# State space mixer's gate product z as seven block products, and the scan's shared value turned once

## The chip, the cores and the metric

The kernel runs on one core of one Trainium2 chip. The metric is the device time of one execution in microseconds, as the median of the runs shown; lower is better. All data are float32. An engine's name stands for itself: TensorE (PE in the profile, with its weight loads as PEld), VectorE (DVE), ScalarE (ACT), GpSimd (POOL) and SyncE (SP).

## The reference, cut to what matters

Two blocks of a network work on 256 latent and 256 context tokens of width 1024. The change touches two mixers of the first block. The state space mixer has eight groups of four heads; z gates its output:

```python
def ssd_mixer(h_lat, h_ctx, ctx_out, w_in, conv_w, conv_b, dt_bias, a_log, d_skip, norm_g, w_out):
    ...
        z, xbc, dt = jnp.split(h @ w_in, [D_INNER, D_INNER + CONV_DIM], axis=-1)
        xbc = jax.nn.silu(dwconv_centred(xbc, conv_w, conv_b))
    ...
    def out(y, z):
        yg = y.reshape(bsz, n, D_INNER).astype(z.dtype) * jax.nn.silu(z)
        yn = rmsnorm(yg.reshape(bsz, n, SSD_GROUPS, D_INNER // SSD_GROUPS), ...)
        return yn.reshape(bsz, n, D_INNER) @ w_out
```

The other is a recurrent scan over the tokens in two directions; both directions read the same v:

```python
def wkv_bidir(prep, s0s):
    r, v, kk, _, dirs = prep
    (df, kf, bf), (db, kb, bb) = dirs
    yf, sf = wkv_scan(r, df, kf, v, kk, bf, s0s[0], False)
    yb, sb = wkv_scan(r, db, kb, v, kk, bb, s0s[1], True)
    return yf + yb, sf, sb
```

## The kernel before

Activations lie feature by feature on 128 partitions, tokens along the free axis. The weights come as 221 tiles of 1 MB in the order of the list PRODUCTS, through a ring of four; SyncE loads tile t when tile t - 4 has been used up (semaphore tiles_used). Products are written to two pairs of PSUM banks in turn; a product may start when the product two before it in the list has been read out, which the semaphores act_emptied and dve_emptied tell. Each engine runs one list of instructions, in the order in which the functions named `..._pe`, `..._dve`, `..._act` and `..._pool` issue them. A float32 matmul stands in the profile as two instructions.

**The state space mixer** (ssd_pe, ssd_dve, ssd_act, ssd_pool) runs one period for each group g. TensorE's list in a period: the first chunk of the product bc of group g + 1 (128 weight columns by 512 tokens, L1861), the decays of group g (L1899), the second chunk of bc (256 tokens), the turns of group g (L1912 to L1918; they wait for both minima and for ScalarE's silu of x and bc), the product z of group g (two chunks of eight matmuls by 256 tokens, L1861), the states and factor rows (L1929, L1938), the first chunk of x of group g + 1, the outputs (L1954 to L1964), the second chunk of x, and one matmul for the norm (L1973). In the last group there is no bc and no x to come: there the first chunk of z stands ahead of the decays, the second behind them, and the turns follow.

VectorE's list in a period: eight conv taps on x of group g (L2148, after ScalarE's copy L2049), the mix of group g - 1 (L2222, L2225, not in group 0), two minima (L2270, after TensorE's decays and a copy by ScalarE, L2094), eight taps on bc of group g + 1, the mask (L2276), four products for the weight matrix (L2281, L2284), the state decays (L2289, which TensorE's outputs wait for), and then, once TensorE's outputs are there (L2238 on), the gate with z's silu (L2251) and a sum (L2253) for the norm. ScalarE does the copies, exponentials, silus and the root; z's silu reads the finished product from PSUM (L2111). GpSimd scales the turned x (L2319) and prepares the next decays (L2309).

**Seven block products** is a form that the MLPs and one more product use already. A tile holds 1024 by 256 weights. Split in halves both ways, weights and tokens give a 2 by 2 block product that takes seven instead of eight block products, each of four matmuls of 128 by 128 weights by 128 tokens (seven_group_pe, L317). VectorE makes four sums of weight blocks beforehand (sums_dve, L368 to L374, each 512 columns; the semaphore mixed tells that they are there, and TensorE waits for it ahead of the third block product), four sums of token blocks once for an input (terms_dve, L390 to L395), and joins the results in four operations (join_dve, L423 to L432) after ScalarE has copied the first of them out of PSUM (first_out_act, L413).

**The scan** (rwkv_scan_pe and its fellows) has eight steps of 64 tokens in each of two directions; the second direction takes the chunks in the order 3, 2, 1, 0, 7, 6, 5, 4. In each step TensorE turns two arrays, V and Q, of each direction, by matmuls with the identity on 64 by 64 pieces (turns, turn_quad, L1432): 32 instructions for a direction. ScalarE copies the two out together, 512 columns (token_rows, L1591, recorded as L1586). Behind the turns stand products that wait for VectorE's transposes (L1679). FIRST_TOUCH = (0, 1, 4, 5) are the steps in which a chunk is met for the first time; in the others the other direction has turned it already.

Of the kernel before, what the change touches and what calls it, by code (L numbers as in the profile page):

```python
# [10 lines left out]
ACT = mybir.ActivationFunctionType  # L11
# [5 lines left out]
SEQ = 256  # L17
CTX = 256
# [23 lines left out]
    *[(f"ssd_{n}{g + d}", 1, 1, by) for g in range(G - 1)  # L42
      for n, d, by in (("bc", 1, "dve"), ("z", 0, "act"), ("x", 1, "dve"))],
    (f"ssd_z{G - 1}", 1, 1, "act"), ("ssd_out", 4, 2, "dve"),
    ("mlp1_up", 16, 1, "dve"), ("mlp1_down", 4, 4, "dve"),
# [168 lines left out]

SEVEN_RUNS = [("mlp0_up", "mlp0_down"), ("mlp1_up", "mlp1_down"), ("gate2", "up2", "down2"), ("hy_mix",)]
TOKENS = {"hy_mix": TOK, "mlp0_up": TOK, "mlp0_down": TOK}
MIX_RUN = 3
RUN_AT, RUN_TILES = {}, []
# [10 lines left out]
FIRST_OUT_AT = {}  # L229
for _run in SEVEN_RUNS[MIX_RUN:] + SEVEN_RUNS[:MIX_RUN]:  # L230
    for _n in _run:
        for _g in range(SHAPE_OF[_n][0]):
            FIRST_OUT_AT[_n, _g] = len(FIRST_OUT_AT) + 1
# [5 lines left out]
def seven_blocks(m, run, n):  # L239

    tile, kt = RUN_TILES[run][n]
    w = m.ring[:, tile % RING, :].rearrange("p (k c n) -> p k c n", k=8, n=P)
    half = kt // 2
    a = [[w[:, half * kh:half * kh + half, c, :] for kh in range(2)] for c in range(2)]
    return tile, half, a, [x[:, 0:half, :] for x in m.weight_sums[run in (1, 2)][n % 2]]

# [110 lines left out]
def sums_dve(s, m, run, n):  # L357

    if run == 0 and 2 <= n < 2 + SIDE_BLOCKS:
        side_block_dve(s, m, n - 2)  # L360
    if n >= len(RUN_TILES[run]):
        return
    dve, sem = s.eng, s.sem
    tile, _, a, w = seven_blocks(m, run, n)
    dve.wait_ge(sem[f"tile_in{tile % RING}"], (tile // RING + 1) * 16)
    if n >= 2:
        dve.wait_ge(sem["tiles_used"], RUN_TILES[run][n - 2][0] + 1)
    dve.tensor_tensor(w[0], a[1][0], a[1][1], ALU.add).then_inc(sem["dve_step"], s.one("dve_step"))  # L368
    dve.tensor_tensor(w[2], a[0][0], a[1][0], ALU.subtract)
    dve.wait_ge(sem["dve_step"], s.made("dve_step"))  # L370
    dve.tensor_tensor(w[1], w[0], a[0][0], ALU.subtract).then_inc(sem["dve_step"], s.one("dve_step"))
    dve.wait_ge(sem["dve_step"], s.made("dve_step"))
    if run or n < 16:
        dve.tensor_tensor(w[3], a[0][1], w[1], ALU.subtract).then_inc(sem["mixed"], s.one("mixed"))  # L374
    else:
        dve.tensor_tensor(w[3], a[0][1], w[1], ALU.subtract)
        b, t = down0_inputs(m, n - 16)
        terms_dve(s, b, t, "mixed")
# [19 lines left out]
def first_kept(m, name, g):  # L398

    if name == "mlp0_down":  # L400
        return m.first0[0]
    return m.first0[g % 2] if name in ("mlp0_up", "hy_mix") else m.first[g % 2]

def first_out_act(s, m, name, g):

    act, sem = s.eng, s.sem
    act.wait_ge(sem["first_done"], FIRST_OUT_AT[name, g])
    if name == "mlp0_down":
        act.wait_ge(sem["first_used"], FIRST_OUT_AT[name, g] - 1)  # L410
    elif g >= 2:
        act.wait_ge(sem["first_used"], FIRST_OUT_AT[name, g] - 2)
    act.activation(first_kept(m, name, g), seven_sums(m, name, g, FIRST), ACT.Copy).then_inc(sem["first_out"], 1)  # L413
# [448 lines left out]
def mlp1_up_dve(s, m):  # L862
    dve, sem = s.eng, s.sem
    hid = m.big_hidden(SEQ)
    dve.wait_ge(sem["h_ready"], s.next("h_ready", NORM_ACT * 2))
    dve.wait_ge(sem["h_rest"], s.made("h_rest"))
# [584 lines left out]
def rwkv_scan_pe(s, m):  # L1451
# [17 lines left out]
    def turns(n, ds):  # L1469
        for d in ds:  # L1470
            for hp in range(HP):
                for w, src in enumerate("VQ"):
                    ins = turn_quad(pe, m, m.place(d, 2, w, hp), chunk(n, d, src, hp))
            ins.then_inc(sem["rows_turned"], s.one("rows_turned"))
# [106 lines left out]
def rwkv_scan_act(s, m):  # L1581
# [6 lines left out]
    def token_rows(n, ds):  # L1588
        for d in ds:
            act.wait_ge(sem["rows_turned"], s.next("rows_turned"))  # L1590
            copy(m.tok_vq(d, n), m.half_bank(d, 2)).then_inc(sem["tok_out"], s.one("tok_out"))  # L1591

# [401 lines left out]
def ssd_pe(s, m):  # L1994
# [9 lines left out]
    for g in range(G - 1):  # L2004
# [3 lines left out]
        ssd_turn_pe(s, m, g)  # L2008
        for c in range(2):
            ssd_chunk_pe(s, m, f"ssd_z{g}", c, SEQ)  # L2010
        ssd_states_pe(s, m, g)
# [4 lines left out]
    g = G - 1  # L2016
    ssd_chunk_pe(s, m, f"ssd_z{g}", 0, SEQ)
    ssd_decays_pe(s, m, g)
    ssd_chunk_pe(s, m, f"ssd_z{g}", 1, SEQ)
    ssd_turn_pe(s, m, g)  # L2020
# [48 lines left out]
def ssd_act(s, m):  # L2069
# [17 lines left out]
    for g in range(G):  # L2087
# [20 lines left out]
        if g < G - 1:  # L2108
            conv_silu_act(s, m, f"ssd_bc{g + 1}", m.conv_bc(g + 1))
        wait_product(s, f"ssd_z{g}", 0)  # L2110
        act.activation(m.z_silu, m.pairs[:, GROUP_AT[f"ssd_z{g}", 0] % 2, :, 0:SEQ], ACT.Silu) \  # L2111
            .then_inc(sem["act_emptied"], s.one("act_emptied"))
        act.wait_ge(sem["new_state"], g + 1)
# [116 lines left out]
def ssd_gate_dve(s, m, g):  # L2230
# [18 lines left out]
    dve.tensor_tensor(y, y, far[:, 0, :], ALU.add).then_inc(sem["dve_step"], s.one("dve_step"))  # L2249
    dve.wait_ge(sem["dve_step"], s.made("dve_step"))  # L2250
    dve.tensor_tensor(m.y_now, m.y_now, m.z_silu, ALU.mult).then_inc(sem["y_gated"], 1)  # L2251
    dve.wait_ge(sem["ssd_squares"], g + 1)
    dve.tensor_tensor(m.y_sq[:, 0, :], m.y_sq[:, 0, :], m.y_sq[:, 1, :], ALU.add).then_inc(sem["y_gated"], 1)  # L2253

def ssd_dve(s, m):
    dve, sem = s.eng, s.sem
    ssd_dt_dve(s, m)
    conv_taps_dve(s, m, "ssd_bc0", bc_chunks(m, 0))
    ssd_tokens_dve(s, m)  # L2260
    dve.wait_ge(sem["ssd_consts"], 16)
    masks = m.ssd_masks.rearrange("p (d t) -> p d t", d=2)[:, None, :, :].broadcast_to([P, 2, 2, P])
    for g in range(G):
        conv_taps_dve(s, m, f"ssd_x{g}", x_chunks(m, g))
        if g:
            ssd_mix_dve(s, m, g - 1)
        for c in range(2):
            dve.wait_ge(sem["seg_kept"], 2 * g + c + 1)
# [9 lines left out]
        for c in range(2):  # L2278
# [5 lines left out]
            dve.tensor_tensor(w, w, m.cbm[:, c, 1:2, :].broadcast_to([P, HPG, P]), ALU.mult) \  # L2284
                .then_inc(sem["w_ready"], 1)
        dve.wait_ge(sem["state_out"], g + 1)
        for dr in range(2):
# [850 lines left out]
class Memory:  # L3138

    def __init__(self, nc, ctx):
# [241 lines left out]
    def tok_v(self, d, n):  # L3383
        return self.tok_vq(d, n)[:, 0:256].rearrange("p (h n) -> p h n", h=HP)

# [438 lines left out]
```

## Time and profile before

| | us |
|---|---|
| runs of the kernel before | 2139.05, 2139.24, 2146.56 |
| median | 2139.24 |
| profiled execution | 2142.77 |
| its span, first to last instruction | 2141.0 |
| TensorE busy in the span | 2091.7 (98%) |
| VectorE busy | 1271.6 (59%) |
| ScalarE busy | 512.0 (24%) |
| GpSimd busy | 159.9 (7%) |

The profiled execution is one of many and lies 3.5 us above the median of the runs. Its times start at the span's beginning. A duration in the timeline of TensorE runs to the modelled end of the last matmul in the row, so the start of the next row tells better how long the row kept TensorE.
### The profile page before, as it was taken

Reading aid. Unit: us, or ns where it says so; the run is one execution under the profiler, and the core shown is the slowest. Engines: PE = TensorE matmul, PEld = TensorE weight load, DVE = VectorE, ACT = ScalarE, POOL = GpSimd, SP = SyncE. Lnnn points to the kernel's source line nnn. Section 1 sums busy time; section 2 is a strip of 40 time slices with the busy share of each in tenths; the row PEclk is TensorE's granted clock in tenths of the full one; section 3 lists DMA queues with packets and bytes.
Section 4 is the critical chain, followed back from the end, with each engine's and each line's share of the span. In section 5 each row is a group of like instructions: output and inputs, shape, how many; then the busy total and the mean of one; then the engine's idle time right before and its main releaser. Section 6 shows DMA issues by size and latency. Waiting matters only on the chain.

```text
span 2141.0 us, 39541 instructions
## 1 busy us (share of the span) xinstructions
PE 2091.7 (98%) x17242; PEld 1701.4 (79%) x17242; DVE 1271.6 (59%) x2425; ACT 512.0 (24%) x1068; POOL 159.9 (7%) x180
## 2 busy tenths in 40 slices
PE   8999899999999999999999999999999999999999
PEld 5854688985588888885666667899998877789999
DVE  4647654444576778766555555388543554239874
ACT  2224732221200000004443444100012243402100
POOL 0002132220000000000221122000001000000000
PEclk9999999999999999999999999999999999999999
DMA  8221022211333334343221222445445522344543
GB/s 337 87 79 60 21 82 82 76 60 51 146 128 127 139 121 148 118 140 135 79 79 59 79 79 75 157 165 183 164 172 197 197 92 87 118 147 148 178 170 126
DMA packets 40693, 261.70 MB, mean 122 GB/s; under 512 B 4919, under 2 KB 6599, under 8 KB 11848
## 3 DMA queue, kind: packets, MB, share of 16 engines
q1 hardware_dynamic: 36720, 249.59, 32.3%
q10 hardware_dynamic: 2904, 6.40, 0.8%
q0 software_dynamic: 896, 3.18, 0.4%
q8 instruction: 136, 2.23, 0.4%
q14 instruction: 37, 0.30, 0.0%
HBM read 257.54 MB, written 1.08 MB: 121 GB/s over the span
## 4 chain that ended last, share of the span: by engine, by line
PE 54%; DVE 1%; ACT 0%; issue 0%; ACTq 0%; DVEq 0%
PE pairs L317 16%; PE pairs L1861 12%; PE pairs L186 9%; PE pairs L2898 4%; PE bank L317 3%; PE pairs L1988 1%; PE pairs L2826 1%; PE bank L1964 1%; PE bank L1954 1%; PE bank L2810 1%; PE bank L1929 1%; PE bank L1899 1%; PE bank L1938 0%; PE bank L2404 0%; PE bank L1912 0%; PE bank L1956 0%
## 5 line engine op out<-in xcount | busy, mean ns | idle before, releaser
L1861 PE MATMUL pairs<-h_sb,ring_sb 128*128 128x512 f32 (+1 forms) x784 | 264.3, 492 | 0.0
L1861 PEld LDWEIGHTS pairs<-h_sb,ring_sb 128*128 128x128 f32 x784 | 147.6, 191 | 105.6 <-issue 94.5
L186 PE MATMUL pairs<-h_sb,ring_sb 128*128 128x256 f32 (+1 forms) x720 | 221.6, 466 | 0.9 <-DVE h_sb L708 0.9
L186 PEld LDWEIGHTS pairs<-h_sb,ring_sb 128*128 128x128 f32 x720 | 135.3, 190 | 84.4 <-issue 72.7
L317 PE MATMUL pairs<-mid 128*128 128x128 f32 (+1 forms) x1304 | 197.1, 306 | 0.0
L317 PEld LDWEIGHTS pairs<-mid 128*128 128x128 f32 x1304 | 179.4, 191 | 10.1
L317 PE MATMUL bank<-mid 128*128 128x256 f32 x544 | 122.0, 379 | 0.0
L317 PE MATMUL pairs<-h_sb,ring_sb 128*128 128x128 f32 (+1 forms) x784 | 118.2, 303 | 3.3 <-ACT h_sb L622 2.7
L317 PEld LDWEIGHTS bank<-mid 128*128 128x128 f32 x544 | 103.4, 190 | 14.1
L317 PEld LDWEIGHTS pairs<-h_sb,ring_sb 128*128 128x128 f32 x784 | 105.8, 193 | 10.9 <-ACT h_sb L622 2.9
L368 DVE TENSOR_TENSOR mid<-ring_sb 128x512 f32<-128x512 f32 (+1 forms) x105 | 71.7, 683 | 67.5 <-PE pairs L317 40.1
L2148 DVE SCALAR_TENSOR_TENSOR big<-pairs,vec_table,big 128x508 f32<-128x508 f32 (+3 forms) x128 | 76.9, 675 | 51.3 <-ACT big L2049 51.2
L317 PE MATMUL pairs<-mid,ring_sb 128*128 128x128 f32 (+1 forms) x520 | 91.2, 318 | 0.0
L186 PE MATMUL pairs<-big,ring_sb 128*128 128x256 f32 x416 | 90.4, 379 | 0.5 <-DVE big L2963 0.5
L2898 PE MATMUL pairs<-h_sb,ring_sb 128*128 128x256 f32 x384 | 89.6, 383 | 0.0
L186 PEld LDWEIGHTS pairs<-big,ring_sb 128*128 128x128 f32 x416 | 79.0, 190 | 11.5 <-DVE big L2963 0.8
L317 PE MATMUL pairs<-big,ring_sb 128*128 128x256 f32 (+1 forms) x472 | 86.6, 331 | 0.0
L317 PEld LDWEIGHTS pairs<-mid,ring_sb 128*128 128x128 f32 x520 | 78.0, 191 | 5.6
L317 PEld LDWEIGHTS pairs<-big,ring_sb 128*128 128x128 f32 x472 | 75.0, 191 | 6.6
L2898 PEld LDWEIGHTS pairs<-h_sb,ring_sb 128*128 128x128 f32 x384 | 70.5, 190 | 12.3 <-issue 3.9
L317 PE MATMUL pairs<-big,mid 128*128 128x128 f32 x648 | 76.9, 275 | 0.0
L317 PEld LDWEIGHTS pairs<-big,mid 128*128 128x128 f32 x648 | 74.6, 192 | 0.0
(550 smaller groups left out, 3617.2 us busy)
## 6 DMA issues: line engine op xcount, KB each, us to landing
ring_sb<-weights SPq DMA_DIRECT2D x221, 1024.0 KB, 4.8
lora_w<-side SPq DMA_DIRECT2D x32, 512.0 KB, 3.3
x_sb<-tokens ACTq DMA_DIRECT2D x1, 2048.0 KB, 12.1
mid<-bias_table POOLq DMA_DIRECT2D x1, 1536.0 KB, 6.9
const_table<-consts ACTq DMA_DIRECT2D x1, 1200.0 KB, 9.0
const_table<-cond_rows SPq DMA_DIRECT2D x1, 1024.0 KB, 10.8
mid<-bias_table POOLq DMA_DIRECT2D x1, 1024.0 KB, 12.7
out<-x_sb ACTq DMA_DIRECT2D x4, 256.0 KB, 2.6
```

The source lines that it names most:

```text
L186: last = pe.matmul(out, w[:, k, c, :], rhs(j * kt + k), start=(j == 0 and k == 0), stop=(j * kt + k == k_end - 1))
L317: ins = pe.matmul(seven_sums(m, name, g, place), left[:, k, :], right[:, k, :], start=(j == 0 and k == 0), stop=(j == tpg - 1 and k == hal ...
L368: dve.tensor_tensor(w[0], a[1][0], a[1][1], ALU.add).then_inc(sem["dve_step"], s.one("dve_step"))
L1861: ins = pe.matmul(m.pairs[:, at % 2, c, 0:T], w[:, k, c, :], m.h[:, k, TOK - T:TOK], start=(k == 0), stop=(k == 7))
L1899: ins = pe.matmul(m.bank[:, 2 * c + dr, :], m.cs_keys[rows, CTX + c * L:CTX + c * L + L], m.cs_heads[c][rows, :], start=True, stop=True)
L1929: ins = pe.matmul(m.bank[:, 0, SEQ * dr:SEQ * dr + SEQ], m.b_tok[:, tt, :], m.xdt_end[:, dr, tt, :], start=(tt == 0), stop=(tt == 1))
L1954: pe.matmul(out, m.states[:, far, dr, cols], lat, start=True, stop=not far)
L1964: ins = pe.matmul(m.bank[64 * side:64 * side + 64, 3, SEQ * j + P * c:SEQ * j + P * c + P], m.xdt[:, dr, c, 64 * h:64 * h + 64], m.wmat[:, ...
L1988: ins = pe.matmul(m.pairs[:, at % 2, c, 0:SEQ], w[:, k % 8, c, :], m.y_fm[:, k, :], start=(k == 0), stop=(k == 15))
L2148: ins = dve.scalar_tensor_tensor(out[:, :, a:b], src[:, :, a + o:b + o], m.vec("conv_w")[:, k + 32 * tap:k + 32 * tap + 1], out[:, :, a:b] ...
L2810: ins = pe.transpose(m.bank[0:n, 2 + side, at:at + P], m.probs2[:, t % 2, side, lo:lo + n], m.const("ident"))
L2898: ins = pe.matmul(m.pair4[:, 2 + g % 2, c * SEQ:c * SEQ + SEQ], w[:, k, c, :], m.h[:, k, CTX:TOK], start=(k == 0), stop=(k == 7))
```

## The change

The product z becomes a fifth run of seven block products (Z_RUN) with sums, terms and a first product of its own in SBUF. VectorE makes the four sums for z of group g behind the mix and ahead of the minima; a sum may start when the tile of z of the group before has been used. It makes the four terms once, ahead of the first x taps, and the join behind the weight matrix' products, ahead of the state decays. ScalarE copies the first product where silu was; silu now runs in place on the joined z behind the exponentials of the factors, and the gate waits for it. In the last group TensorE issues the decays after the fourth block product. In the scan V is turned and copied only in the steps of FIRST_TOUCH, and the other steps read the copy that the other direction made. The second MLP's wait for h_ready is split in two, since the mixer now waits for the first half of its count.

```diff
-      for n, d, by in (("bc", 1, "dve"), ("z", 0, "act"), ("x", 1, "dve"))],
-    (f"ssd_z{G - 1}", 1, 1, "act"), ("ssd_out", 4, 2, "dve"),
+      for n, d, by in (("bc", 1, "dve"), ("z", 0, "dve"), ("x", 1, "dve"))],
+    (f"ssd_z{G - 1}", 1, 1, "dve"), ("ssd_out", 4, 2, "dve"),
-SEVEN_RUNS = [("mlp0_up", "mlp0_down"), ("mlp1_up", "mlp1_down"), ("gate2", "up2", "down2"), ("hy_mix",)]
+SEVEN_RUNS = [("mlp0_up", "mlp0_down"), ("mlp1_up", "mlp1_down"), ("gate2", "up2", "down2"), ("hy_mix",),
+              tuple(f"ssd_z{g}" for g in range(G))]
@@ sums_dve
+    kept = 1 if run == Z_RUN else 2
+    if n >= kept:
+        dve.wait_ge(sem["tiles_used"], RUN_TILES[run][n - kept][0] + 1)
@@ mlp1_up_dve
-    dve.wait_ge(sem["h_ready"], s.next("h_ready", NORM_ACT * 2))
+    dve.wait_ge(sem["h_ready"], s.next("h_ready", NORM_ACT))
@@ rwkv_scan_pe, turns
-                for w, src in enumerate("VQ"):
-                    ins = turn_quad(pe, m, m.place(d, 2, w, hp), chunk(n, d, src, hp))
+                if n in FIRST_TOUCH:
+                    turn_quad(pe, m, m.place(d, 2, 0, hp), chunk(n, d, "V", hp))
+                ins = turn_quad(pe, m, m.place(d, 2, 1, hp), chunk(n, d, "Q", hp))
@@ rwkv_scan_act, token_rows
-            copy(m.tok_vq(d, n), m.half_bank(d, 2)).then_inc(sem["tok_out"], s.one("tok_out"))
+            if n in FIRST_TOUCH:
+                copy(m.tok_v(d, n), m.part(d, 2, 0))
+            copy(m.tok_q(d, n), m.part(d, 2, 1)).then_inc(sem["tok_out"], s.one("tok_out"))
+def ssd_z_pe(s, m, g, between=None):
+    pe, sem = s.eng, s.sem
+    if g == 0:
+        pe.wait_ge(sem["terms"], s.next("terms", 4))
+    seven_group_pe(s, m, f"ssd_z{g}", 0, lambda j: (halves(m.h[:, :, CTX:TOK], 0, 4), m.z_terms), between=between)
@@ ssd_pe
-        for c in range(2):
-            ssd_chunk_pe(s, m, f"ssd_z{g}", c, SEQ)
+        ssd_z_pe(s, m, g)
...
     g = G - 1
-    ssd_chunk_pe(s, m, f"ssd_z{g}", 0, SEQ)
-    ssd_decays_pe(s, m, g)
-    ssd_chunk_pe(s, m, f"ssd_z{g}", 1, SEQ)
+    ssd_z_pe(s, m, g, between=lambda n, last: None if last else ssd_decays_pe(s, m, g))
     ssd_turn_pe(s, m, g)
@@ ssd_act
-        wait_product(s, f"ssd_z{g}", 0)
-        act.activation(m.z_silu, m.pairs[:, GROUP_AT[f"ssd_z{g}", 0] % 2, :, 0:SEQ], ACT.Silu) \
-            .then_inc(sem["act_emptied"], s.one("act_emptied"))
+        first_out_act(s, m, f"ssd_z{g}", 0)
...
         ins.then_inc(sem["factors"], 1)
+        act.wait_ge(sem["dve_emptied"], EMPTIED_BEFORE[f"ssd_z{g}"] + 1)
+        act.activation(m.z_silu, m.z_silu, ACT.Silu).then_inc(sem["ssd_squares"], 1)
@@ ssd_gate_dve
+    dve.wait_ge(sem["ssd_squares"], 2 * g + 1)
     dve.tensor_tensor(m.y_now, m.y_now, m.z_silu, ALU.mult).then_inc(sem["y_gated"], 1)
@@ ssd_dve
+    terms_dve(s, halves(m.h[:, :, CTX:TOK], 0, 4), m.z_terms)
...
         if g:
             ssd_mix_dve(s, m, g - 1)
+        sums_dve(s, m, Z_RUN, g)
...
+        join_dve(s, m, f"ssd_z{g}", 0, quarters(m.z_silu), "dve_emptied")
         dve.wait_ge(sem["state_out"], g + 1)
@@ Memory.tok_v
-        return self.tok_vq(d, n)[:, 0:256].rearrange("p (h n) -> p h n", h=HP)
+        made_by, slot = (d, (0, 1, 0, 0, 1, 0)[n]) if n in FIRST_TOUCH else (1 - d, {2: 1, 3: 0, 6: 0, 7: 1}[n])
+        return self.scan[made_by]["vq"][slot][:, 0:256].rearrange("p (h n) -> p h n", h=HP)
```

## Rows read from the trace of the kernel before

**Rows 1.** The page's first part: busy time of TensorE, share of span, instructions.
```profile
PE 2091.7 (98%) x17242; PEld 1701.4 (79%) x17242; DVE 1271.6 (59%) x2425; ACT 512.0 (24%) x1068; POOL 159.9 (7%) x180
```

**Rows 2.** By stretch (scan; mixer period): us, busy PE, PEld, DVE, ACT, POOL; clock, DMA.
```profile
263.90:492.00 228.10, 215.54 (x6576) 202.94 (x6577) 109.81 (x287) 65.80 (x166) 59.27 (x80) 0.99 0.21 77
...
1093.40:1136.60 43.20, 43.20 (x193) 27.62 (x192) 24.35 (x36) 18.27 (x25) 8.39 (x7) 1.00 0.21 73
```

**Rows 3.** Timeline of TensorE in one period: start, us, instruction, count, idle before.
```profile
1105.82 1.04 PE L1912 MATMUL bank<-const_table,big 128*128 128x128 f32 x8
...
1107.78 7.07 PE L1861 MATMUL pairs<-h_sb,ring_sb 128*128 128x256 f32 x32
1114.69 1.89 PE L1929 MATMUL bank<-mid,big 128*128 128x256 f32 x8
...
1117.57 7.13 PE L1861 MATMUL pairs<-h_sb,ring_sb 128*128 128x512 f32 x16
```

**Rows 4.** Timeline of VectorE in the same period: taps, mix, minima.
```profile
1094.64 5.33 DVE L2148 SCALAR_TENSOR_TENSOR big<-pairs,vec_table,big 128x508 f32<-128x508 f32 x8 [3.29 <-ACT big L2049]
...
1101.67 0.88 DVE L2225 SCALAR_TENSOR_TENSOR big<-big,vec_table 128x256 f32<-128x256 f32 x2
1102.46 1.28 DVE L2270 TENSOR_TENSOR mid<-bank,mid 128x512 f32<-128x512 f32 x2
```

**Rows 5.** Timeline of TensorE, then VectorE, in the last group.
```profile
1309.51 3.62 PE L1861 MATMUL pairs<-h_sb,ring_sb 128*128 128x256 f32 x16
1313.05 1.99 PE L1899 MATMUL bank<-big,const_table 64*128 64x512 f32 x8
...
1320.01 1.06 PE L1912 MATMUL bank<-const_table,big 128*128 128x128 f32 x8 [1.32 <-DVE mid L2270]
...
1318.58 1.28 DVE L2270 TENSOR_TENSOR mid<-bank,mid 128x512 f32<-128x512 f32 x2
```

**Rows 6.** The chain that ended last, in the second MLP: start, us, instructions.
```profile
1496.28 3.57 PE pairs L317 x32
```

**Rows 7.** Timeline of VectorE in the second MLP: first and last sum, join's first.
```profile
1396.15 0.68 DVE L368 TENSOR_TENSOR mid<-ring_sb 128x512 f32<-128x512 f32 x1
...
1398.07 0.69 DVE L374 TENSOR_TENSOR mid<-ring_sb,mid 128x512 f32<-128x512 f32 x1
1399.84 0.42 DVE L423 TENSOR_TENSOR big<-pairs,mid 128x256 f32<-128x256 f32 x1 [1.07 <-PE pairs L317]
```

**Rows 8.** Timeline of GpSimd, VectorE and ScalarE in the period of rows 3.
```profile
1108.59 3.04 POOL L2319 TENSOR_TENSOR mid<-big,root 128x768 f32<-128x768 f32 x3 [34.83 <-ACT big L2104]
...
1113.21 1.42 DVE L2284 TENSOR_TENSOR mid<-mid,big 128x512 f32<-128x512 f32 x1
...
1129.33 1.29 DVE L2238 TENSOR_TENSOR lt<-bank,mid 128x512 f32<-128x512 f32 x2 [11.13 <-PE bank L1964]
...
1133.48 0.63 ACT L2121 ACTIVATE big<-big 128x512 f32<-128x512 f32 x1 [13.87 <-DVE big L2251]
```

**Rows 9.** Busy TensorE by stretch: stretch, us, busy (instructions), clock, DMA.
```profile
224.80:231.60 6.80, 5.50 (x23) 0.50 0.00 0
...
341.00:344.20 3.20, 2.17 (x56) 1.00 0.68 282
344.30:347.60 3.30, 3.30 (x69) 0.50 0.03 7
...
1317.00:1320.40 3.40, 2.08 (x12) 1.00 0.25 39
```

**Rows 10.** Timeline of TensorE and VectorE in the scan, turns and a transpose.
```profile
402.38 1.10 PE L1432 MATMUL pairs<-const_table,big 64*64 64x64 f32 x32
403.31 0.63 PE L1432 MATMUL bank<-big,lt 64*64 64x64 f32 x16
...
371.72 0.31 PE L1432 MATMUL bank<-const_table,big 64*64 64x64 f32 x4
...
372.44 0.45 DVE L1679 STREAM_TRANSPOSE big<-const_table 128x256 f32<-128x256 f32 x1
```

More of the change, by code:

```diff
@@ L212, in product_empty @@
         empty(m.pairs[:, GROUP_AT[name, g] % 2], g)
-SEVEN_RUNS = [("mlp0_up", "mlp0_down"), ("mlp1_up", "mlp1_down"), ("gate2", "up2", "down2"), ("hy_mix",)]
+SEVEN_RUNS = [("mlp0_up", "mlp0_down"), ("mlp1_up", "mlp1_down"), ("gate2", "up2", "down2"), ("hy_mix",),
+              tuple(f"ssd_z{g}" for g in range(G))]
 TOKENS = {"hy_mix": TOK, "mlp0_up": TOK, "mlp0_down": TOK}
-MIX_RUN = 3
+MIX_RUN, Z_RUN = 3, 4
 RUN_AT, RUN_TILES = {}, []
@@ L229 @@
 FIRST_OUT_AT = {}
-for _run in SEVEN_RUNS[MIX_RUN:] + SEVEN_RUNS[:MIX_RUN]:
+for _run in [SEVEN_RUNS[n] for n in (MIX_RUN, 0, Z_RUN, 1, 2)]:
     for _n in _run:
@@ L244, in seven_blocks @@
     a = [[w[:, half * kh:half * kh + half, c, :] for kh in range(2)] for c in range(2)]
-    return tile, half, a, [x[:, 0:half, :] for x in m.weight_sums[run in (1, 2)][n % 2]]
+    sums = m.z_sums if run == Z_RUN else m.weight_sums[run in (1, 2)][n % 2]
+    return tile, half, a, [x[:, 0:half, :] for x in sums]
 BANKS = {FIRST: (0, 1), SECOND: (0, 2), SIXTH: (0, 3), THIRD: (1, 0), FIFTH: (1, 1), SEVENTH: (1, 2), FOURTH: (1, 3)}
@@ L365, in sums_dve @@
     dve.wait_ge(sem[f"tile_in{tile % RING}"], (tile // RING + 1) * 16)
-    if n >= 2:
-        dve.wait_ge(sem["tiles_used"], RUN_TILES[run][n - 2][0] + 1)
+    kept = 1 if run == Z_RUN else 2
+    if n >= kept:
+        dve.wait_ge(sem["tiles_used"], RUN_TILES[run][n - kept][0] + 1)
     dve.tensor_tensor(w[0], a[1][0], a[1][1], ALU.add).then_inc(sem["dve_step"], s.one("dve_step"))
@@ L401, in first_kept @@
         return m.first0[0]
+    if name.startswith("ssd_z"):
+        return m.z_first
     return m.first0[g % 2] if name in ("mlp0_up", "hy_mix") else m.first[g % 2]
@@ L408, in first_out_act @@
     act.wait_ge(sem["first_done"], FIRST_OUT_AT[name, g])
-    if name == "mlp0_down":
+    if name == "mlp0_down" or name.startswith("ssd_z"):
         act.wait_ge(sem["first_used"], FIRST_OUT_AT[name, g] - 1)
@@ L2250, in ssd_gate_dve @@
     dve.wait_ge(sem["dve_step"], s.made("dve_step"))
+    dve.wait_ge(sem["ssd_squares"], 2 * g + 1)
     dve.tensor_tensor(m.y_now, m.y_now, m.z_silu, ALU.mult).then_inc(sem["y_gated"], 1)
-    dve.wait_ge(sem["ssd_squares"], g + 1)
+    dve.wait_ge(sem["ssd_squares"], 2 * g + 2)
     dve.tensor_tensor(m.y_sq[:, 0, :], m.y_sq[:, 0, :], m.y_sq[:, 1, :], ALU.add).then_inc(sem["y_gated"], 1)
@@ L2260, in ssd_dve @@
     ssd_tokens_dve(s, m)
+    dve.wait_ge(sem["h_ready"], s.next("h_ready", NORM_ACT))
+    dve.wait_ge(sem["h_rest"], s.made("h_rest"))
+    terms_dve(s, halves(m.h[:, :, CTX:TOK], 0, 4), m.z_terms)
     dve.wait_ge(sem["ssd_consts"], 16)
@@ L3267, in __init__ @@
         self.y_far = self.lt_flat.rearrange("p (d n) -> p d n", d=2)
+        self.z_sums = [mid[:, 7296 + 512 * n:7808 + 512 * n].rearrange("p (k c) -> p k c", k=4) for n in range(4)]
+        self.z_terms = four_terms(mid, 9344)
+        self.z_first = mid[:, 11392:11520]
         self.sp2, self.end_rows = mid[:, 6656:7168], mid[:, 7168:7296]
```

## The prediction

> **What bounds the kernel now.** I read the engines' totals first: TensorE is busy for 98% of the span [rows 1]. That is an average, so the second view is the busy time by stretch [rows 2]. In one period of the state space mixer, which handles one group of heads, TensorE works 43.20 of 43.20 us and VectorE 24.35; in the scan TensorE works 215.54 of 228.10. TensorE's own instructions pace both stages, and work taken from it there counts in full, provided no other engine comes late. So the third view is the timeline of one period, for how close the others are: TensorE [rows 3] against VectorE [rows 4].
>
> The loop runs like this. A conv product x ends; ScalarE copies; VectorE runs eight conv taps (5.33 us from 1094.64), the mix of the previous group (L2222, L2225, ending at 1102.55), and two minima (L2270, 1102.46 to 1103.74). TensorE meanwhile does a chunk of bc, the decays and another chunk of bc, and at 1105.82 begins the turns (L1912), which wait for the second minimum. In the last group, where it really did wait, the turns began 0.15 us after the minimum ended (1318.58 + 1.28 = 1319.86, then 1320.01) [rows 5]. So in groups 1 to 6 the minimum has 1105.82 - 0.15 - 1103.74 = **1.93 us to spare**. This is the number that the change has to fit into.
>
> **The product z.** Before, z is 16 matmuls of 256 columns, each two instructions: 32 instructions from 1107.78 to 1114.69, 6.91 us [rows 3]. After, it is 28 matmuls of 128 columns, 56 instructions. The MLP does the same block products at 3.57 us for 32 instructions, 0.1116 us each [rows 6], so 56 x 0.1116 = 6.25. The saving is 0.66 us a group, 5.3 us in eight groups at the very most.
>
> **VectorE's sums.** Four operations of 512 columns: in the MLP from 1396.15 to 1398.07 + 0.69 = 1398.76, 2.61 us [rows 7]. The next operation starts some 0.07 before the fourth ends, so they push what follows by 2.54. They stand between the mix and the minima, on exactly the chain above. Groups 1 to 6: the second minimum ends at 1102.46 + 2.54 + 1.28 = 1106.28, the turns begin at 1106.43 instead of 1105.82, a stall of 0.61. Against the 0.66 saved that leaves 0.05 a period, -0.3 us for six. Queued behind the sums are the minima, and for them wait ScalarE's exponentials and its bc copies, VectorE's bc taps and the w products, all about 1 us later. GpSimd begins 0.85 to 1 us later too, so what it shares with VectorE moves along [rows 8]. Bounds for the stall: 0 (shorter hand-offs) to 1.2 (each of the four sums 0.15 us longer than in the MLP, about one hand-off). Group 0 has no mix, whose 2.58 us (from the taps' end at 1099.97 to 1102.55) the sums replace, so its turns start on time and it keeps the full -0.66.
>
> **The join, the terms, silu.** The join's four operations last at most 0.42 us each, as in the MLP at 1399.84 [rows 7]: 1.7 us, behind the w products. Behind it are queued the state decays, which TensorE's outputs await after the next x chunk (1117.57 to about 1124.6) [rows 3]. VectorE is idle for 11.13 us before 1129.33 [rows 8], that is from 1118.20; with 1 us of delay and the join the decays end near 1120.9. Hidden by 3.7 us; uncovered it would cost 1.7 a group. The four terms (2.6 us, once) go ahead of the first x taps, where VectorE idles about as long as ahead of these taps, 3.29 us [rows 4]: hidden. Doubled by GpSimd they would be 2 us late, about what group 0 has to spare. On ScalarE a copy of the first product takes the place of silu; silu goes behind the factors with one more table load, 1.28 + 0.6 us, into an idle time of 13.87 us before the square [rows 8]. The gate now waits for it, about 10 us after it is done. The h_ready wait of the second MLP only splits a count; nothing. SP's tile queue sees the z tile released 0.05 us earlier, in the last group some 8 us later, for a tile needed over 20 us after that.
>
> **The last group is different.** There z is not behind the turns but before them, in the very place where TensorE has nothing else. Now: first chunk from 1309.51, decays, second chunk, a wait of 1.32, turns at 1320.01 [rows 5]. After: two block products (16 x 0.1116 = 1.79) to 1311.30; then TensorE must have the sums, and these come after the taps of x7 and mix 6, in place of the minimum at 1318.58: done at 1321.19, TensorE goes on at 1321.34 after **10 us of idle**. Then two products 1.79, the decays 1.92, three products 2.68: the turns at 1327.73. The minima (decays end 1325.05, then a copy of 0.6 and a minimum of 0.69) are ready by 1326.7 and no longer late; what is late is TensorE's own remaining work. Cost 1327.7 - 1320.0 = **+7.7**, bounds 7.0 to 8.4.
>
> **The clock after that idle.** The granted clock by stretch [rows 9]: near 224.8, where attention keeps TensorE waiting, it stands at 0.50 (1.2 GHz, against 2.4 at 1.00) for 6.8 us; in the scan it is 1.00 until 344.2, with TensorE idle for 1.03 of 3.20 us, and then 0.50 for 3.3. After 1.32 us of idle in the last group (1317.0 to 1320.4) it stayed at 1.00. No row shows 10 us. I take 3.4 us of work at half rate, +1.7, by the scan's row, the only one with dense work behind the wait; bounds 0 (it falls and returns while TensorE idles) and 3.4 (6.8 us at half rate).
>
> **The scan.** In four of eight steps the value is not turned: 16 of 32 instructions for each direction. One direction's 32 take from 402.38 to 403.31, 0.93 us [rows 10]. Four steps x two directions x 0.465 = **-3.7 us**. What comes late next? The products behind the turns wait for VectorE's transposes: in the step at 371.72 the second ends at 372.89 [rows 10]; with turns of 0.93 the first direction's products would start at 372.65 and the second's at 373.12, still later. ScalarE's copies of 512 columns become 256 in the four steps, and two of 256 in the other four, 0.2 us longer, on an engine that works 65.80 of 228.10 us here [rows 2]. Bounds -5.6 (a shortened turn falls into a half-clock stretch, or a wait for instructions goes) to -1.9 (half is taken by hand-offs).
>
> **Sum.** -0.66 - 0.3 + 7.7 + 1.7 - 3.7 = +4.7. The profiled execution took 2142.8 us, so it would be 2147.5; it lies 3.5 above the median of the runs, 2139.2, so on that scale **2144**.
>
> **Rivals.**
> (1) *The minima absorb the sums*: the stall in groups 1 to 6 is 0, all 0.66 remain, -3.7 more: 2140. Against it stand the 1.93 us to spare for 2.54.
> (2) *The scan gives nothing*, its steps being held by the exchange between engines: +3.7, 2147.6. For it: TensorE is only 94% busy there; against it, the waits before the turned products are shorter than the cut leaves room for.
> (3) *Slower: the clock falls in every period.* If a stall of 0.6 us before the turns is enough, each of six periods runs 3.4 us at half rate: 6 x 1.7 = +10.2, 2154, 0.7% slower. It decides from whether half rate follows waits below 1 us in dense work. For it: half rate followed 1.03 us of waiting for instructions in the scan [rows 9]. Against: 1.32 us in the last group left the clock at 1.00.
> The Trainium skill speaks for it: "TensorE: Matmul & The Clock Gate", section "A second HAM failure mode: psum-queue depth-cycling", tells of a kernel whose short idles between groups of matmuls made the clock swing and cost throughput. By that rule it is 2154, by the row of the last group 2144; the row is from this kernel's own matmuls and I go by it.
> (4) *Slower: the sums cost double*, as VectorE's two-input operations do beside GpSimd (L2284, 1.42 us for 512 columns) [rows 8]: +2.5 x 6 = 15, 2159. Against: GpSimd starts at 1108.59, after the sums.
> (5) *Faster*: the cut in instructions also removes the scan's waits for instructions, about 1 us a step: -8, 2136.
>
> **How the numbers follow.** Forecast 0.60; rival 1 0.13, rival 2 0.11, rival 3 0.06, rival 4 0.04, rival 5 0.06. The cost bounds added up give 2136 to 2152; with rivals 1, 2 and the likelier half of 5, 2137 to 2151. This kernel's measurement can tell 0.5%, 10.7 us, from no change: slower by that needs rivals 3 or 4, or everything bad at once (0.10); faster by that has no mechanism that reaches it (0.03); 0.87 between.
>
> **What would show it.** In the changed profile: z 6.25 us in a period; periods 43.15 long with a wait of about 0.6 before L1912, released by the minima; one idle of about 10 us before the last group's third block product, released by the sums, with the clock at 0.50 behind it; turns of the scan 0.94 instead of 1.87 us in four steps, and about 3.7 us less in the scan. I am wrong if the mixer doesn't become longer overall, if the last group's idle is under 7 us, or if half-clock stretches show in the periods.

## The result, and the profile of the changed kernel

| | before | after |
|---|---|---|
| median of 20 runs each, us | 2140.78 | 2144.12 |
| lowest to highest, us | 2136.01 to 2146.56 | 2141.23 to 2153.95 |
| profiled execution, us | 2142.77 | 2146.78 |
| its span, us | 2141.0 | 2145.0 |

After takes 1.0023 times as long as before (95% interval 1.0015 to 1.0032), that is 4.9 us longer, between 3.2 and 6.9. This ratio is not the quotient of the two medians, which lie only 3.3 us apart. The sum had +4.7, and 2144 as the time. That 2144 met the median to 0.1 us is luck: it started from 2139.2, the median of three runs, and the longer series puts before at 2140.8.

The totals hide where this happens. TensorE is busy for 2.3 us less than in [rows 1], VectorE for 35 us more.

```profile
PE 2089.4 (97%) x17306; PEld 1701.5 (79%) x17306; DVE 1306.6 (61%) x2493; ACT 520.1 (24%) x1090; POOL 159.6 (7%) x180
```

The busy time by stretch of after: the scan, a period of the mixer, and three stretches of the last group; us, then busy PE, PEld, DVE, ACT, POOL, then granted clock, DMA share, GB/s.

```profile
267.10:492.40 225.30, 214.75 (x6578) 202.54 (x6576) 110.40 (x288) 64.71 (x174) 59.05 (x80) 0.99 0.21 78
1061.00:1104.20 43.20, 42.76 (x218) 27.73 (x217) 28.39 (x45) 19.74 (x27) 8.38 (x7) 1.00 0.22 75
1307.00:1316.80 9.80, 0.04 (x1) 0.00 (x0) 9.71 (x15) 3.43 (x4) 0.00 (x0) 0.66 0.19 81
1316.90:1320.30 3.40, 3.40 (x16) 3.40 (x16) 0.00 (x0) 0.00 (x0) 0.00 (x0) 0.50 0.00 0
1320.40:1323.80 3.40, 3.40 (x22) 2.08 (x21) 1.34 (x2) 1.85 (x3) 0.00 (x0) 1.00 0.00 0
```

Against [rows 2], the period is as long as before, but TensorE now idles for 0.44 us of it and VectorE works 4 us more. In the last group TensorE does nothing for 9.80 us, then works for 3.4 us at a granted clock of 0.50 and after that at 1.00.

One period of after, TensorE's timeline (start, us, instruction, count, idle before), the counterpart of [rows 3]:

```profile
1058.95 1.06 PE L1928 MATMUL bank<-const_table,big 128*128 128x128 f32 x8 [0.44 <-DVE mid L2288]
...
1060.94 1.95 PE L319 MATMUL pairs<-h_sb,ring_sb 128*128 128x128 f32 x16
...
1067.19 1.89 PE L1945 MATMUL bank<-mid,big 128*128 128x256 f32 x8
...
1102.15 1.07 PE L1928 MATMUL bank<-const_table,big 128*128 128x128 f32 x8 [0.44 <-DVE mid L2288]
```

The turns (L1928, L1912 before) now wait for the second minimum. The product z takes from 1060.94 to 1067.19, 6.25 us where it took 6.91, and the turns come again after 43.20 us.

VectorE in the same period, for [rows 4], then its join and its state decays, for [rows 7] and [rows 8]:

```profile
1047.17 5.33 DVE L2161 SCALAR_TENSOR_TENSOR big<-pairs,vec_table,big 128x508 f32<-128x508 f32 x8 [3.29 <-ACT big L2062]
...
1055.00 0.68 DVE L371 TENSOR_TENSOR mid<-ring_sb 128x512 f32<-128x512 f32 x1
...
1056.92 0.69 DVE L377 TENSOR_TENSOR mid<-ring_sb,mid 128x512 f32<-128x512 f32 x1
1057.53 1.28 DVE L2288 TENSOR_TENSOR mid<-bank,mid 128x512 f32<-128x512 f32 x2
...
1070.78 0.41 DVE L428 TENSOR_TENSOR big<-pairs,mid 128x256 f32<-128x256 f32 x1
...
1072.46 0.76 DVE L2308 TENSOR_TENSOR mid<-mid,root 128x256 f32<-128x256 f32 x2
1081.83 1.29 DVE L2251 TENSOR_TENSOR lt<-bank,mid 128x512 f32<-128x512 f32 x2 [8.62 <-PE bank L1980]
```

The sums go from 1055.00 to where the minima begin, 1057.53: they push the minima by 2.53. The second minimum ends at 1058.81, and the turns follow 0.14 later. The join takes 1.68 (1070.78 to 1072.46), and behind it VectorE still idles for 8.62 us.

The last group, TensorE and then VectorE, for [rows 5]:

```profile
1305.10 1.95 PE L319 MATMUL pairs<-h_sb,ring_sb 128*128 128x128 f32 x16
1316.84 3.72 PE L319 MATMUL pairs<-mid 128*128 128x128 f32 x16 [9.80 <-DVE mid L377]
1320.49 1.99 PE L1915 MATMUL bank<-big,const_table 64*128 64x512 f32 x8
...
1325.19 1.04 PE L1928 MATMUL bank<-const_table,big 128*128 128x128 f32 x8
...
1316.09 0.69 DVE L377 TENSOR_TENSOR mid<-ring_sb,mid 128x512 f32<-128x512 f32 x1
```

From the start of z to the turns it is 1325.19 - 1305.10 = 20.09 us, where it was 1320.01 - 1309.51 = 10.50 [rows 5]. These **9.59 us** are more than the whole loss; the rest of the change gains.

The scan, for [rows 10]: turns of both directions in a step that doesn't turn the value, and the products behind them; then the first row of the scan and the first behind it, and the same two in before.

```profile
318.07 0.66 PE L1437 MATMUL bank<-const_table,mid 64*64 64x64 f32 x16
...
319.03 0.63 PE L1437 MATMUL bank<-big,lt 64*64 64x64 f32 x16
...
267.17 1.15 PE L1437 MATMUL bank<-mid 64*64 64x64 f32 x32
...
492.93 3.70 PE L1746 MATMUL bank<-h_sb,const_table 128*128 128x512 f32 x8 [0.59 <-DVE h_sb L1701]
```
```profile
263.94 1.15 PE L1432 MATMUL bank<-mid 64*64 64x64 f32 x32
...
496.55 3.70 PE L1738 MATMUL bank<-h_sb,const_table 128*128 128x512 f32 x8 [0.59 <-DVE h_sb L1693]
```

The turns take 319.03 - 318.07 = 0.96 us for both directions; 0.93 for each, 1.86 for both, was read in [rows 10]. From the scan's first row to the first behind it lie 225.76 us; in before they are 232.61 us apart.

**Where the time went, profile against profile.** The scan begins 3.2 us later (267.17 against 263.94), in an opening that the change doesn't touch; it is 6.8 us shorter; from the first turns of the mixer to the last (1015.79 to 1325.19 against 1019.38 to 1320.01) it is 8.8 us longer; what follows is 1.2 us shorter, where before had a stretch of 3.6 us at a clock of 0.53 (1392.0 to 1395.6) and after has 1.00. Together +4.0, the difference of the two spans. The first and the last of these four belong to the executions (in the eleven profiles of this document the scan begins anywhere between 262.9 and 269.3 us, behind the same opening), so the two middle ones need runs of their own.

### The profile page after: what moved, and what is told of

Same layout as the page of the kernel before. It is cut to its first block, busy times and chain, and to the rows that moved or that the text cites. A ratio compares the mean times of both kernels' runs of the same rounds, so it can differ in the third digit from the quotient of the medians.

```text
span 2145.0 us, 39799 instructions
## 1 busy us (share of the span) xinstructions
PE 2089.4 (97%) x17306; PEld 1701.5 (79%) x17306; DVE 1306.6 (61%) x2493; ACT 520.1 (24%) x1090; POOL 159.6 (7%) x180
## 4 chain that ended last, share of the span: by engine, by line
PE 50%; DVE 4%; issue 0%; ACT 0%; ACTq 0%; DVEq 0%
PE pairs L319 18%; PE pairs L186 8%; PE pairs L1869 7%; PE pairs L2917 4%; PE bank L319 3%; DVE big L2161 2%; PE pairs L2004 1%; PE pairs L2845 1%; PE bank L1980 1%; PE bank L1970 1%; PE bank L2829 1%; PE bank L1945 1%; DVE big L2235 1%; PE bank L1954 0%; PE bank L1928 0%
## 5 line engine op out<-in xcount | busy, mean ns | idle before, releaser
L319 PE MATMUL pairs<-mid 128*128 128x128 f32 (+1 forms) x1496 | 221.8, 304 | 9.8 <-DVE mid L377 9.8
L319 PEld LDWEIGHTS pairs<-mid 128*128 128x128 f32 x1496 | 203.2, 193 | 20.9 <-DVE mid L377 10.0
L1869 PE MATMUL pairs<-h_sb,ring_sb 128*128 128x512 f32 (+1 forms) x528 | 207.6, 547 | 0.0
L186 PEld LDWEIGHTS pairs<-h_sb,ring_sb 128*128 128x128 f32 x720 | 135.3, 190 | 84.4 <-issue 72.7
L1869 PEld LDWEIGHTS pairs<-h_sb,ring_sb 128*128 128x128 f32 x528 | 99.1, 191 | 98.4 <-issue 93.8
L319 PE MATMUL pairs<-h_sb,ring_sb 128*128 128x128 f32 (+1 forms) x912 | 132.9, 297 | 3.3 <-ACT h_sb L627 2.7
L319 PEld LDWEIGHTS pairs<-h_sb,ring_sb 128*128 128x128 f32 x912 | 120.3, 191 | 11.5 <-ACT h_sb L627 3.3
L371 DVE TENSOR_TENSOR mid<-ring_sb 128x512 f32<-128x512 f32 (+1 forms) x113 | 77.0, 682 | 67.9 <-PE pairs L319 40.2
L319 PE MATMUL pairs<-mid,ring_sb 128*128 128x128 f32 (+1 forms) x584 | 99.6, 313 | 0.0
L319 PEld LDWEIGHTS pairs<-mid,ring_sb 128*128 128x128 f32 x584 | 85.8, 191 | 5.6
L2917 PEld LDWEIGHTS pairs<-h_sb,ring_sb 128*128 128x128 f32 x384 | 70.5, 190 | 12.2 <-issue 3.9
L372 DVE TENSOR_TENSOR mid<-ring_sb 128x512 f32<-128x512 f32 (+1 forms) x113 | 76.7, 678 | 0.0
```

The costliest lines, as they stand in the source:

```text
L186: last = pe.matmul(out, w[:, k, c, :], rhs(j * kt + k), start=(j == 0 and k == 0), stop=(j * kt + k == k_end - 1))
L319: ins = pe.matmul(seven_sums(m, name, g, place), left[:, k, :], right[:, k, :], start=(j == 0 and k == 0), stop=(j == tpg - 1 and k == hal ...
L1869: ins = pe.matmul(m.pairs[:, at % 2, c, 0:T], w[:, k, c, :], m.h[:, k, TOK - T:TOK], start=(k == 0), stop=(k == 7))
L2917: ins = pe.matmul(m.pair4[:, 2 + g % 2, c * SEQ:c * SEQ + SEQ], w[:, k, c, :], m.h[:, k, CTX:TOK], start=(k == 0), stop=(k == 7))
```

## The experiments

Each ratio is to the kernel before, with its 95% interval. Before ran beside the experiments, with a median of 2140.63 us in the first four and of 2138.99 in the next three; the ratios are again not the quotients of the medians.

**The scan alone.** The kernel before with the scan's part of the change and nothing else.

```diff
-                for w, src in enumerate("VQ"):
-                    ins = turn_quad(pe, m, m.place(d, 2, w, hp), chunk(n, d, src, hp))
+                if n in FIRST_TOUCH:
+                    turn_quad(pe, m, m.place(d, 2, 0, hp), chunk(n, d, "V", hp))
+                ins = turn_quad(pe, m, m.place(d, 2, 1, hp), chunk(n, d, "Q", hp))
...
```

> The kernel before with the scan's part of the change alone (V turned and copied only in four of eight steps). Theory A, the sum's: the scan becomes 3.7 us shorter (64 matmuls fewer, 0.93 us in each of four steps), the kernel 2140.8 - 3.7 = 2137.1, ratio 0.9983. Theory B, from the changed kernel's profile, whose scan is 6.8 us shorter (225.2 against 232.0): the cut also takes away waits for instructions, ratio 0.9968. Theory C: the scan is held by the exchange between engines, ratio 1.000. In the profile A has the four steps without V about 0.6 to 1.1 us shorter and the others unchanged but for waits for instructions.

2134.47 us, 0.998 (0.9969 to 0.9990): -4.3 us, between -6.6 and -2.1; by the two medians it is -6.2. The -3.7 of the sum lies inside, and that the scan gives nothing (rival 2) is out. The prediction's waits for instructions are idle time of TensorE that the profile puts down to "issue", which means that it shows nothing that was waited for. In the scan they are (engine, line, us in total, times, longest), in before, in after and in this kernel:

```profile
PE bank L1432 <- issue: 5.8, 7, 1.4
PE pairs L1432 <- issue: 3.4, 3, 1.8
```
```profile
PE bank L1437 <- issue: 3.9, 5, 1.4
PE pairs L1437 <- issue: 3.3, 3, 1.4
```
```profile
PE bank L1432 <- issue: 6.6, 7, 2.6
PE pairs L1432 <- issue: 2.0, 3, 1.0
```

9.2, 7.2 and 8.6 us: they have not gone, as they would by rival 5. The profiled scan of this kernel takes 228.99 us, 3.6 less than before's and 3.2 more than after's, whose scan has the same work.

**The product alone.** The changed kernel with the scan as it was before, the diff above the other way round.

> The changed kernel with the scan put back as before, so the mixer's part alone. The sum's theory: -0.66 in group 0, -0.3 in groups 1 to 6, +7.7 in the last group and +1.7 for the clock, together +8.4, ratio 1.0039; the changed kernel's profile reads +9.0, ratio 1.0042. The rival that the mixer's part costs nothing and the loss is elsewhere: ratio 1.000. Periods of 43.2 us, a wait of 9.8 us in the last group.

2150.59 us, 1.0042 (1.0028 to 1.0056): +9.0 us, between 6.0 and 12.0, where the sum has +8.4; by the two medians it is +10.0. In its profile the mixer takes 1332.90 - 1022.32 = 310.58 us from its first turns to its last, 9.95 more than before's 300.63. By the ratios the two parts add up: 9.0 - 4.3 = +4.7, and the whole change measured +4.9. The profiled scan takes 230.25 us here, 2.4 less than before's with the same turns.

**The sums ahead of the taps, in the last group.** All else is as in the changed kernel.

```diff
+        if g == G - 1:
+            sums_dve(s, m, Z_RUN, g)
         conv_taps_dve(s, m, f"ssd_x{g}", x_chunks(m, g))
         if g:
             ssd_mix_dve(s, m, g - 1)
-        sums_dve(s, m, Z_RUN, g)
+        if g < G - 1:
+            sums_dve(s, m, Z_RUN, g)
```

> The changed kernel, but in the last group alone VectorE makes the sums for z ahead of the conv taps of x instead of behind the mix. If the last group's wait and the clock after it are the whole loss: the wait of 9.8 us and the half clock go, the turns of the last group begin 9.7 to 10 us earlier, the kernel takes 2144.1 - 9.8 = 2134.3, ratio to before 0.997. If TensorE's 10 us of idle only hid another lateness (the minima), at most half of that comes back: above 2139, ratio above 0.999. In the profile a wait for the minima of about 2 us should stand in front of the last group's turns in place of the 9.8.

2135.17 us, 0.997 (0.9959 to 0.9980): -6.4 us, where the change as it stands is +4.9. The wait of 9.80 us for the sums isn't there; TensorE's one long wait in the last group is again that for the minima. Timeline of TensorE, start of z and turns:

```profile
1303.29 1.95 PE L319 MATMUL pairs<-h_sb,ring_sb 128*128 128x128 f32 x16
...
1313.79 1.06 PE L1928 MATMUL bank<-const_table,big 128*128 128x128 f32 x8 [1.98 <-DVE mid L2291]
```

From z to the turns it is 10.50 us, just as before: in this group VectorE's taps, mix and minima set that time, so the shorter product only makes the wait longer (1.98 against 1.32). Other groups are unchanged (43.20 a period).

**The sums ahead of the taps, in all groups.**

```diff
+        sums_dve(s, m, Z_RUN, g)
         conv_taps_dve(s, m, f"ssd_x{g}", x_chunks(m, g))
         if g:
             ssd_mix_dve(s, m, g - 1)
-        sums_dve(s, m, Z_RUN, g)
```

> The changed kernel with VectorE's sums for z ahead of the conv taps of x in all groups, where VectorE idles 3.29 us. Theory: the sums (2.6 us) fit into that idle time, so the stall of 0.6 us ahead of the turns goes in groups 1 to 6 and the last group's wait goes too: periods of 42.56 instead of 43.20 us, 3.6 us less than with the last group's sums alone moved, the kernel 2130.7, ratio to before 0.9953. Rival: the sums delay the taps and with them the whole chain (the gate of the group before is not yet done when TensorE ends x), then the periods stay at 43.2 or grow, and the ratio is 0.997 or more.

2131.96 us, 0.9956 (0.9944 to 0.9968): **9.4 us faster than before**, some 14 faster than the change as it stands (12 by the medians), and the fastest kernel here. VectorE and TensorE in its timeline:

```profile
1039.42 0.69 DVE L377 TENSOR_TENSOR mid<-ring_sb,mid 128x512 f32<-128x512 f32 x1
1040.87 5.33 DVE L2161 SCALAR_TENSOR_TENSOR big<-pairs,vec_table,big 128x508 f32<-128x508 f32 x8 [0.76 <-ACT big L2062]
...
1052.05 1.04 PE L1928 MATMUL bank<-const_table,big 128*128 128x128 f32 x8
...
1094.62 1.04 PE L1928 MATMUL bank<-const_table,big 128*128 128x128 f32 x8
```

The sums need only the weights, and they fit into the time in which VectorE waits for ScalarE's copy ahead of the taps: of its 3.29 us, 0.76 are left. The turns no longer wait in these groups, and the period is 42.57 us where it was 43.22 before: all of z's 0.66 us arrives.

**The clock behind the long wait.** The changed kernel, with 20 useless products on TensorE in the last group, ahead of z, where it would idle.

```diff
-                   m.z_terms), between=between)
+                   m.z_terms), between=between,
+                   before=(lambda j: busy_pe(s, m, m.bank[:, 3, :], 20)) if g == G - 1 else None)
```

> The changed kernel with twenty matmuls of 128 x 128 by 256 columns that serve nothing ahead of the last group's z: 20 x 0.432 = 8.6 us, inside the 9.8 us that TensorE waits there. If the half clock behind the wait comes from TensorE's idling, it goes: the two block products after the wait take 1.8 us instead of 3.7, the products behind them 2.7 instead of 2.9, the last group's period 48.2 instead of 50.3 us, the kernel 2144.1 - 2.1 = 2142, ratio to before 1.0013. If the half clock has another cause: period 50.3, ratio 1.0023. The granted clock from the wait's end on is to be 1.00 or 0.50.

2141.82 us, 1.0017 (1.0008 to 1.0025); the interval overlaps that of the change, so the times alone don't settle 1.7 us. The timeline and the stretch behind the wait do:

```profile
1299.39 8.80 PE L460 MATMUL bank<-const_table 128*128 128x256 f32 x40
...
1311.14 2.05 PE L319 MATMUL pairs<-mid 128*128 128x128 f32 x16 [1.17 <-DVE mid L377]
...
1317.82 1.04 PE L1929 MATMUL bank<-const_table,big 128*128 128x128 f32 x8
```
```profile
1311.10:1314.50 3.40, 3.36 (x22) 1.00 0.02 5
```

TensorE still has to wait for VectorE's sums, but it is idle for only 1.17 us, and the clock is 1.00 when it goes on. So the half clock followed from the idling. From there to the turns it takes 6.68 us, against 1325.19 - 1316.84 = 8.35 in the change: in that execution the clock costs **1.67 us**. The rest of the loss is the wait itself.

The product alone has the same idle of 9.80 us, and there the half clock reaches into the decays (line 1912 of that kernel, 3.07 us, where line 1915 of after has 1.99):

```profile
1311.66 1.95 PE L319 MATMUL pairs<-h_sb,ring_sb 128*128 128x128 f32 x16
1323.40 3.78 PE L319 MATMUL pairs<-mid 128*128 128x128 f32 x16 [9.80 <-DVE mid L377]
1327.11 3.07 PE L1912 MATMUL bank<-big,const_table 64*128 64x512 f32 x8
...
1332.90 1.04 PE L1925 MATMUL bank<-const_table,big 128*128 128x128 f32 x8
```

From the wait's end to the turns it takes 9.50 us. In the four kernels below that keep this wait it takes 8.93 (four operations more), 9.38 (one), 8.58 (two) and 9.40 (a longer join). So the clock's price behind one and the same idle was 1.67 to 2.82 us in six executions, and the change's is the lowest of them.

**Longer sums in groups 1 to 6.** Four, one and two more operations of 512 columns on VectorE, chained behind the sums; their results are not used.

```diff
         sums_dve(s, m, Z_RUN, g)
+        if 0 < g < G - 1:
+            more_dve(s, m, 4)
```

> The changed kernel with four more VectorE operations of 128 x 512 in a chain (0.72 us each, 2.9 together, results not used) right behind the sums in groups 1 to 6. If nothing is to spare any more between the sums and the turns, as the sum has it, every us counts: periods of 43.2 + 2.85 = 46.05 us, six of them +17, the kernel 2161. If the stall of 0.6 comes from elsewhere and the sums still have room: less than 2.2 us a period.

2175.16 us (two runs), 1.0171 (1.0153 to 1.0188), 14 us above what was expected. Four operations take 2.87 us and the wait at the turns grows by as much, from 0.44 to 3.35; below, the first wait, and the stretch behind it:

```profile
1062.31 1.45 PE L1928 MATMUL bank<-const_table,big 128*128 128x128 f32 x8 [3.35 <-DVE mid L2297]
```
```profile
1062.90:1066.20 3.30, 3.30 (x14) 2.94 (x13) 2.21 (x5) 2.35 (x4) 0.54 (x1) 0.50 0.07 30
```

The first period, up to this wait, is 46.08 us, 2.9 above the change's. Each later one is 47.77, 1.69 more again: the price of the half clock, which follows each of the six waits. So there is no cover for VectorE's time here, and rival 3's mechanism is real, with its price of 1.7 a period; only it didn't set in with the change's waits.

> The changed kernel with one more VectorE operation (0.72 us, result not used) behind the sums in groups 1 to 6. The last run with four of them had waits of 3.35 us ahead of the turns and the granted clock at 0.50 behind each from the second on, 1.7 us a period on top of the 2.9. This run asks from where that rival decides. If a wait of 1.15 us is too short for it: periods 43.2 + 0.7 = 43.9 us, clock 1.00. If not: up to 45.6.

> The same with two more operations (1.44 us). If a wait of 1.9 us is too short for the clock to fall: periods 44.6 us, clock 1.00. If it is enough: up to 46.3 us, with 0.50 behind the waits.

One run each: 2147.87 and 2153.16 us (before beside them: 2142.69). Waits of TensorE at the turns (us in total, times, longest) and the stretch of the periods; first with one, then with two operations more:

```profile
PE bank L1928 <- DVE mid L2297: 7.0, 6, 1.2
```
```profile
1015.00:1300.00 285.00, 278.02 (x1428) 181.14 (x1427) 186.97 (x290) 126.03 (x166) 57.08 (x48) 1.00 0.20 71
```
```profile
PE bank L1928 <- DVE mid L2297: 11.3, 6, 1.9
```
```profile
1015.00:1300.00 285.00, 273.66 (x1395) 178.63 (x1395) 188.68 (x291) 126.03 (x166) 57.63 (x49) 1.00 0.20 71
```

Six waits of 1.2 us and six of 1.9 leave the clock at 1.00 in all periods; the periods are 43.9 and 44.65 us, longer by the waits alone.

**A longer join.** Three more operations on VectorE behind the join; their results are not used.

```diff
         join_dve(s, m, f"ssd_z{g}", 0, quarters(m.z_silu), "dve_emptied")
+        more_dve(s, m, 3)
```

> The changed kernel with three more VectorE operations of 128 x 512 in a chain (2.2 us, results not used) right behind the join in all eight groups. If the join and the decays behind it are hidden by 3.7 us, as the sum has it, the periods stay at 43.2 us and the kernel at 2144. If the join is on the path, 2.2 x 8 = +17, 2161.

2144.08 us, 1.0020 (1.0010 to 1.0030), as the change. Timeline of VectorE and TensorE:

```profile
1068.82 2.15 DVE L2273 TENSOR_TENSOR mid<-mid 128x512 f32<-128x512 f32 x3
1071.00 0.76 DVE L2316 TENSOR_TENSOR mid<-mid,root 128x256 f32<-128x256 f32 x2
...
1073.40 0.61 PE L1970 MATMUL bank<-big,mid 128*128 128x128 f32 x4
```

2.15 us more, and the periods are still 43.20: the decays end at 1071.76, 1.64 before the outputs that need them. The join is off the path with room left.

## Why the prediction came out

**z.** 56 x 0.1116 = 6.25 by the MLP's rate; 6.25 measured.

**The sums in groups 1 to 6.** Right in mechanism and in size. Foreseen was a push of 2.54 against 1.93 us to spare, a stall of 0.61, and 0.05 left of each 0.66. The push is 2.53, the hand-off 0.14 instead of 0.15, and a period is 43.20 where it was 43.22. The trace shows an idle of 0.44 rather than 0.61, since it counts from the modelled end of the matmuls ahead; from the periods, 0.66 saved and 0.02 left make a stall of 0.64. Rival 1 (the minima absorb the sums, 2140) falls with it, and becomes true only when the sums move ahead of the taps. Rival 4 (double price beside GpSimd, 2159) falls too: the sums take 0.68 to 0.69 each. What longer sums cost is seen with four operations more: 2175, above that rival's 2159, since the clock joins in.

**The last group.** The step that a view of the steady periods would not have shown, and the largest term. Forecast: an idle of 10 us, the turns 7.7 later, 1.7 for the clock, together 9.4. Measured in after: 9.80, and 9.59 together, 1.67 of them the clock; in the product alone 9.80 again, and 1332.90 - 1311.66 = 21.24 from z to the turns, 10.74 more than before. The minima are no longer late there, as foreseen; what is late is TensorE's own remaining work. Moving the sums of this one group takes the loss away.

**The clock.** That half rate follows the idle, and dense work then pays for it, is shown by the useless products. Its size was right in part by luck. In after the stretch of work at half rate is 3.4 us long, the length taken from the scan's row [rows 9]; but the prediction called that row the only one with dense work behind a wait, and the same trace has one of twice the length, behind an idle of 1.90 us ahead of the mixer:

```profile
968.90:975.70 6.80, 6.78 (x19) 0.50 0.62 260
```

So 3.4 was a choice between two lengths, and five other executions with the same idle paid 1.90 to 2.82 us and not 1.7, all within the bounds of 0 and 3.4. Rival 3 (half rate in every period, 2154) gave the right price for a period and was wrong that a stall of 0.6 us suffices: neither that nor waits of 1.2 and 1.9 us in every period brought it about, while waits of 3.35 did each time. No single length marked the point in these runs, as the last section shows. The rule of the Trainium skill that stood beside it ("TensorE: Matmul & The Clock Gate", section "A second HAM failure mode: psum-queue depth-cycling", short idles between groups of matmuls make the clock swing) agrees with the trace of the kernel with waits of 3.35 us, where each period lost 1.69 us, and not with the change, whose periods stood at 1.00 throughout.

**Join, terms, silu.** Hidden, as said. The decays end at 1073.22 and are needed at 1077.05, 3.8 us later; 3.7 was forecast. Silu's table load (1.28 us) and its 0.63 lie in ScalarE's idle time, of which 11.93 us are left before the square. In group 0 the terms run ahead of the first taps; the first of them takes 1.52 us beside GpSimd, and they end at 1005.22, just as the taps begin; ScalarE's copy that the taps need ended only at 1005.00. Group 0's turns are not late.

**The scan.** Forecast -3.7, with bounds -5.6 to -1.9. By their ratios the two timed comparisons, with and without the product, give -4.3 and -4.1 (1.0023 against 1.0042); by their medians -6.2 and -6.5. The turns were cut by 0.9 us in each of four steps, 3.6 us, as worked out. The profiles say more than that: with all turns the scan took 232.61 and 230.25 us in two executions; with the cut ones it took 228.99 us where the scan alone was changed, and 223.49 to 225.76 us in the eight other kernels. So the term is probably too small, and perhaps beyond its bounds. Rival 5 may have a part of the rest: the waits for instructions were 9.2 and 7.8 us with all turns, and 6.0 to 8.6 us in the nine executions with the cut ones. How much of it is the change, and why the kernel with the scan alone kept the longer scan, stays open.

**The sum.** +4.7 forecast, +4.9 (3.2 to 6.9) measured. The terms of the mixer came in at +8.8 in after and +9.95 in the product alone, against +8.4, and the scan gave probably more than its 3.7. These two misses go against each other, so the sum is closer than its terms, and that much is luck. That the two profiled spans differ by only 4.0 says little: 3.2 in the opening and -1.2 behind the mixer lie outside what the change touches.

## What to carry to other kernels

Here an exchange of TensorE's work for VectorE's paid only where VectorE had the time. For a kernel of your own: read the chain from VectorE to the next matmul, subtract, and look for an idle stretch ahead of the chain for whatever needs only weights. That one line, moved, turned 0.23% slower into 0.44% faster. Look separately at the first and the last turn of a loop: when the last has another order of work, it can cost more than all the others give.

## What the runs showed of the hardware that was not expected

The length of a wait did not by itself decide the clock behind it. In one execution of each kernel, a wait of 1.98 us ahead of the last group's turns, with the same instructions around it, was followed by a clock of 1.00 when only the last group's sums were moved, and by 0.50 when all were moved (the stretch behind the wait, us, busy TensorE, PEld, DVE, ACT, POOL, clock, DMA, GB/s; first the one, then the other):

```profile
1313.80:1317.20 3.40, 3.40 (x21) 3.14 (x22) 1.19 (x2) 2.33 (x6) 0.65 (x1) 1.00 0.65 270
```
```profile
1306.00:1309.20 3.20, 3.20 (x13) 2.82 (x12) 0.00 (x0) 1.44 (x3) 0.13 (x1) 0.50 0.55 230
```

Twelve waits of 1.2 and 1.9 us were followed by 1.00, and six of 3.35 by 0.50. Nor did the price follow from the length: the idle of 9.80 us cost 1.67 to 2.82 us in six executions. From the turns to the end of the products behind them it is 1321.82 - 1313.79 = 8.03 us in the one and 1315.24 - 1305.54 = 9.70 in the other: a wait of about 2 us cost 1.67 us more in one order of the same work, and nothing more in the other. What decided it isn't settled. And the scan, with the same instructions, differed by 2.4 us between two executions with all turns and by 5.5 among nine with the cut ones; a term of that size can't be read from one pair of profiles.
